# Strassen's seven products on six k-tiles of the feed-forward input instead of four, plain units mixed among them, and the activations split in the output stage

## The reference

```
x = x + 0.5 * SwiGLU_1(rms_norm(x))          # w_in 2048 x (2*5632), w_out 5632 x 2048
h = rms_norm(x); P = h @ w_in                # q, k, v of 8 dilated and 8 differential heads
x = x + concat(attention heads) @ w_out
x = x + 0.5 * SwiGLU_2(rms_norm(x))

def swiglu_ffn(x, g, w_in, w_out):
    h = rms_norm(x, g)
    gate, up = jnp.split(h @ w_in, 2, axis=-1)
    return (jax.nn.silu(gate) * up) @ w_out
```

## Time and profile before

| quantity | value |
|---|---|
| median of three runs | 1860.8 us |
| profiled execution, its own time | 1861.02 us |
| its span | 1859.2 us |
| PE, DVE, ACT busy | 1842.5, 1254.9, 941.3 us |
| DMA | 352.88 MB, 190 GB/s mean |

### The profile page before, as it was taken

One profiled execution on the slowest core, in us unless ns is written; L12 is line 12 of the kernel. 1 busy time (PEld: TensorE's weight loads), 2 busy tenths in 40 slices (PEclk: granted clock), 3 DMA queues, 4 the chain that ended last, 5 costly groups with the idle time before them and its releaser, 6 DMA issues.

```text
span 1859.2 us, 23201 instructions
## 1 busy us (share of the span) xinstructions
PE 1842.5 (99%) x8408; PEld 1529.2 (82%) x8408; DVE 1254.9 (67%) x1432; ACT 941.3 (51%) x1183; POOL 47.8 (3%) x71
## 2 busy tenths in 40 slices
PE   7999999999999999999999999999999999999999
PEld 6888888888888888888888888888888888888887
...
PEclk9999999999999999999999999999999999999999
...
GB/s 296 170 202 198 208 182 205 200 196 188 226 182 180 187 203 198 189 183 155 174 167 181 138 172 167 163 200 209 195 204 201 185 209 193 203 181 182 193 214 114
DMA packets 178888, 352.88 MB, mean 190 GB/s; under 512 B 7312, under 2 KB 7952, under 8 KB 178576
## 3 DMA queue, kind: packets, MB, share of 16 engines
...
...
## 4 chain that ended last, share of the span: by engine, by line
PE 98%; DVE 1%; DMA 0%; ACT 0%; issue 0%; SPq 0%; ACTq 0%
PE acc L391 22%; PE acc L393 22%; PE acc L392 22%; PE acc L495 6%; PE acc L496 6%; PE acc L494 6%; PE turn L435 2%; PE turn L433 2%; PE turn L434 2%; PE turn L418 2%; PE acc L435 1%; PE acc L434 1%; PE acc L433 1%; PE turn L546 1%; PE turn L567 1%; DMA w_raw<-in_ffn_w_in 0%
## 5 line engine op out<-in xcount | busy, mean ns | idle before, releaser
L894 DVE TENSOR_TENSOR w_lo<-w_raw,w_hi 128x1024 fp32r<-128x1024 f32 x352 | 413.2, 1182 | 395.6 <-ACT w_hi L649 393.3
L649 ACT ACTIVATE w_hi<-w_raw 128x1024 fp32r<-128x1024 f32 x352 | 358.7, 1021 | 460.0 <-PE acc L393 439.6
L663 ACT ACTIVATE w_hi<-w_raw 128x1024 fp32r<-128x1024 f32 (+1 forms) x400 | 402.9, 1017 | 363.6 <-PE acc L496 131.3
L903 DVE TENSOR_TENSOR w_lo<-w_raw,w_hi 128x1024 fp32r<-128x1024 f32 (+1 forms) x400 | 460.4, 1168 | 151.6 <-ACT w_hi L663 146.1
L391 PE MATMUL acc<-w_hi,h_hi 128*128 128x512 f32 x992 | 392.1, 395 | 1.8 <-DVE w_lo L894 1.8
L393 PE MATMUL acc<-w_hi,h_lo 128*128 128x512 f32 x992 | 387.1, 390 | 0.0
L392 PE MATMUL acc<-w_lo,h_hi 128*128 128x512 f32 x992 | 386.9, 390 | 0.0
L391 PE MATMUL acc<-w_hi,act_hi 128*128 128x512 f32 x704 | 274.3, 390 | 0.0
L393 PE MATMUL acc<-w_hi,act_lo 128*128 128x512 f32 x704 | 273.9, 389 | 0.0
L392 PE MATMUL acc<-w_lo,act_hi 128*128 128x512 f32 x704 | 273.9, 389 | 0.0
L391 PEld LDWEIGHTS acc<-w_hi,h_hi 128*128 128x128 f32 x992 | 186.8, 188 | 42.0 <-issue 4.8
...
## 6 DMA issues: line engine op xcount, KB each, us to landing
w_raw<-in_ffn_w_in SPq DMA_DIRECT2D x176, 1024.0 KB, 5.0
w_raw<-in_ffn_w_out SPq DMA_DIRECT2D x64, 1024.0 KB, 4.9
w_raw<-in_w_in SPq DMA_DIRECT2D x48, 1024.0 KB, 5.0
...
w_raw<-in_w_out SPq DMA_DIRECT2D x16, 1024.0 KB, 4.9
...
```

What stands on the lines that cost most here:

```text
L649: nc.scalar.activation(w_hi[:, v % RING, 0:count, :], w_raw[:, v // 2 % RAW, k0:k0 + count, :], ACT.Copy).then_inc(hi_ready, 1)
L663: nc.scalar.activation(w_hi[:, v % RING, 0:count, :], w_raw[:, piece % RAW, k0:k0 + count, :], ACT.Copy).then_inc(hi_ready, 1)
L894: nc.vector.tensor_tensor(w_lo[:, v % RING, 0:count, :], w_raw[:, v // 2 % RAW, k0:k0 + count, :], w_hi[:, v % RING, 0:count, :].bitcast(F32),
L903: nc.vector.tensor_tensor(w_lo[:, v % RING, 0:count, :], w_raw[:, piece % RAW, k0:k0 + count, :], w_hi[:, v % RING, 0:count, :].bitcast(F3 ...
```

## The change

Each half of the Strassen block has three k-tiles instead of two (`KS = 3`), and ten k-tiles stay plain (`K_PLAIN`). A product is now two units, of 2 and of 1 k-tile, with 9 matmuls in all. An iteration has 24 units: 10 plain ones (120 matmuls) and 14 units of products (63 matmuls), 183 in all. `IN_RAW` lists them in order: four plain, P1, P5, a plain one, P2, P6, two plain, P3, P4, P7, three plain.

The raw blocks of the products now have their own buffer, `block_raw`, with five places of 3 k-tiles. Two plain k-tiles of gate and of up go to `odd_raw`. The four weight sums are made with other operands, are 1536 columns wide instead of 1024, and stand at other places of DVE's order. The DMAs of an iteration are ten instead of eight, with the same bytes.

`block_raw`, `s_hi` and `s_lo` lie where `act_hi` lies. So while the input stage runs, hidden activations are only copied (`copy_act`, ACT) to `act_raw`, which is `act_lo`'s memory. They are split later (`round_act`): blocks 0 and 1 in the last iteration, blocks 2 to 9 among the first chunk's units. PE waits for this by `act_ready`. The last iteration is written out behind the loop on ACT and DVE. The factor `rstd` of the up half moves out of `hidden` and into `update_x` (`half_rstd`).

In `activation_sums` the token operands are made from `h_hi + h_lo` with one sum of 1536 columns and four of 384.

```
-IN_UNITS = 20
+KS = 3
+K_PLAIN = KD - 2 * KS
...
+G0, G1, U0, U1, G2, U2, B11, B12, B21, B22, T1 = range(11)
+IN_RAW = ((G0, 0, 2), (G0, 2, 2), (G1, 0, 2), (G1, 2, 2), (B11, 0, 2), (B11, 2, 1), (T1, 0, 2), (T1, 2, 1), (G2, 0, 2),
+          (B21, 0, 2), (B21, 2, 1), (T1, 0, 2), (T1, 2, 1), (U0, 0, 2), (U0, 2, 2), (B22, 0, 2), (B22, 2, 1),
+          (B21, 0, 2), (B21, 2, 1), (B12, 0, 2), (B12, 2, 1), (U1, 0, 2), (U1, 2, 2), (U2, 0, 2))
+IN_UNITS = len(IN_RAW)
+P1, P5, P2, P6, UP, P3, P4, P7, UP_REST = 4, 6, 9, 11, 13, 15, 17, 19, 21
+SUM_OF = {P5: 1, P5 + 1: 1, P6: 2, P6 + 1: 2, P4: 3, P4 + 1: 3, P7: 4, P7 + 1: 4}
+FREED = {G0: 2, G1: 4, B11: 6, G2: 9, U0: 15, B22: 17, B21: 19, B12: 21, U1: 23, U2: 24}
...
+            s_hi = sb("s_hi", [P, 4, KS, P], F32R, sums)
+            s_lo = sb("s_lo", [P, 4, KS, P], F32R, sums)
+            block_raw = sb("block_raw", [P, 5, KS, NC], F32, sums)
+            sums.enter_context(nc.sbuf_tensor("sums_end", [P, KF * SEQ - 2 * 4 * KS * P - 5 * KS * NC], F32))
+            act_raw = sb("act_raw", [P, KF, SEQ], F32, sums)
...
+                for piece in FREED:
+                    if not first:
+                        sp.wait_ge(lo_ready, i * IN_UNITS + (base + FREED[piece]))
+                    elif piece < G2:
+                        sp.wait_ge(lo_ready, UNIT[s_in] + 2 * (piece + len(PARTS_D) + 1))
+                    elif piece in (G2, U2):
+                        sp.wait_ge(rows_ready, ROWS[R_FFN1 if s_in == IN1 else R_FFN2])
+                    elif s_in == IN2:
+                        sp.wait_ge(units_used, UNIT[s_in])
...
+            def form(u0, p, lhs, o, start, stop):
+
+                for v in (p, p + 1):
+                    count = IN_RAW[v][2]
+                    pe.wait_ge(lo_ready, u0 + v + 1)
+                    for kk in range(count):
...
-                for v in range(4, 6):
-                    in_unit(u0, v, 2 * v, UK, 0, False, False)
+                turn_rows(i + r0, 0, splits(r0), None, i + r0)
                 if s_in == IN2:
                     pe.wait_ge(bank_free[2], READS[s_in][2])
-                form(u0, P1, block_of(KD - 4, 0), partial[0], True, True)
+                form(u0, P1, block_of(0, 0), partial[0], True, True)
                 form(u0, P5, sum_of(1), partial[1], True, True)
-                form(u0, P2, block_of(KD - 2, 0), banks[0][:, 0, :], False, True)
+                in_unit(u0, P2 - 1, 2 * KT, 0, (True, True), False)
+                form(u0, P2, block_of(1, 0), banks[0][:, 0, :], False, True)
                 pe.wait_ge(partial_copied, copies + 1)
                 form(u0, P6, sum_of(2), partial[0], True, True)
-                form(u0, P4, block_of(KD - 2, 1), banks[0][:, 1, :], False, True)
-                form(u0, P3, sum_of(4), banks[1][:, 0, :], True, False)
+                for v in range(UP, P3):
+                    in_unit(u0, v, UK * (v - UP), 1, (v > UP, v > UP), False)
+                form(u0, P3, sum_of(4), banks[1][:, 0, :], False, False)
+                form(u0, P4, block_of(1, 1), banks[0][:, 1, :], False, True)
                 pe.wait_ge(partial_copied, copies + 2)
                 form(u0, P7, sum_of(3), partial[0], True, True)
...
+                for v in range(UP_REST, IN_UNITS):
+                    in_unit(u0, v, UK * (v - UP_REST + P3 - UP), 1, (True, True), v == IN_UNITS - 1)
...
+                    for v in range(UNITS_F):
+                        if v == 4 and b < turns:
+                            r = i * 2 + (r0 + IN_LOOPS + b)
+                            turn_rows(r, b, r - (b + IN_LOOPS * (n + 1)), None, r - b)
+                        if v < UNITS_A and v % 2 == 0:
+                            pe.wait_ge(act_ready, IN_LOOPS * n + ACT_NEEDED[v])
+                        if v == UNITS_A:
+                            pe.wait_ge(turn_split, splits(r0 + FFN_ITERS))
+                        chunk(PARTS_F, u0, range(v, v + 1), act, b)
...
+            def copy_act(i, r0):
+
+                act.wait_ge(rows_turned, i + (r0 + 1))
+                nc.scalar.activation(act_raw[:, bass.ds(i * 4, 4), :], turn4[0], ACT.Copy).then_inc(turn_hi, 1)
+
+            def round_act(j):
+
+                nc.scalar.activation(act_hi[:, KT * j:KT * (j + 1), :], act_raw[:, KT * j:KT * (j + 1), :],
+                                     ACT.Copy).then_inc(act_hi_ready, 1)
...
+            def hidden(s_in, i, r0, n):
+
+                split_in_hi(s_in, i, n, 4, 8)
+                copy_act(i, r0)
                 split_in_hi(s_in, i, n, 8, 10)
                 copy_partial(s_in, i)
-                split_in_hi(s_in, i, n, 10, 18)
+                split_in_hi(s_in, i, n, 10, 27)
                 silu(s_in, i)
-                split_in_hi(s_in, i, n, 18, 24)
+                if isinstance(i, int):
+                    for j in range(2):
+                        round_act(j)
+                split_in_hi(s_in, i, n, 27, 28)
...
+                    if c == 0:
+                        round_act(2)
...
+            def round_act(n, j):
+
+                dve.wait_ge(act_hi_ready, IN_LOOPS * n + j + 1)
+                k = slice(KT * j, KT * (j + 1))
+                nc.vector.tensor_tensor(act_lo[:, k, :], act_raw[:, k, :], act_hi[:, k, :].bitcast(F32),
+                                        ALU.subtract).then_inc(act_ready, 1)
...
+                landed = i * 16 + (IN_LOOPS * n + 1) * 16
+                b_11, b_12, b_21, b_22, t_1 = (in_raw(piece) for piece in (B11, B12, B21, B22, T1))
+                dve.wait_ge(block_landed[0], landed)
+                dve.wait_ge(block_landed[1], landed)
+                weight_sum(t_1, b_12, b_11, ALU.subtract)
+                split_in_lo(s_in, i, 4, 9)
+                dve.wait_ge(block_landed[3], landed)
+                dve.wait_ge(sum_ready, sums + 1)
+                dve.wait_ge(lo_ready, i * IN_UNITS + (u0 + P5 + 2))
+                weight_sum(t_1, b_22, t_1, ALU.subtract)
+                split_in_lo(s_in, i, 9, 14)
+                dve.wait_ge(sum_ready, sums + 2)
+                dve.wait_ge(lo_ready, i * IN_UNITS + (u0 + P2 + 2))
+                weight_sum(b_21, b_21, t_1, ALU.subtract)
+                split_in_lo(s_in, i, 14, 15)
+                weight_sum(b_12, b_22, b_12, ALU.subtract)
+                split_in_lo(s_in, i, 15, 17)
+                dve.wait_ge(units_used, i * IN_UNITS + (u0 + P6 + 2))
                 dve.wait_ge(partial_copied, copies + 1)
                 add(rows[:, 1, 0, :], partial[0], rows[:, 0, 0, :]).then_inc(partial_copied, 1)
-                split_in_lo(s_in, i, 13, 16)
-                dve.wait_ge(units_used, i * IN_UNITS + (u0 + P7 + 1))
+                split_in_lo(s_in, i, 17, 25)
+                dve.wait_ge(units_used, i * IN_UNITS + (u0 + P7 + 2))
                 dve.wait_ge(partial_copied, copies + 2)
                 add(rows[:, 0, 1, :], partial[0], rows[:, 1, 0, :]).then_inc(partial_copied, 1)
                 add(rows[:, 1, 0, :], partial[1], rows[:, 1, 0, :])
-                split_in_lo(s_in, i, 16, 17)
                 dve.wait_ge(partial_copied, copies + 3)
                 add(rows[:, 1, 1, :], partial[1], rows[:, 0, 1, :]).then_inc(partial_added, 1)
                 dve.wait_ge(partial_added, done)
                 add(rows[:, 0, :, :], acc[0][:, :, :], rows[:, 0, :, :]).then_inc(bank_free[0], 1)
-                split_in_lo(s_in, i, 17, 24)
+                split_in_lo(s_in, i, 25, 28)
+                if isinstance(i, int):
+                    for j in range(2):
+                        round_act(n, j)
                 dve.wait_ge(units_used, i * IN_UNITS + (u0 + IN_UNITS))
                 add(rows[:, 1, :, :], acc[1][:, :, :], rows[:, 1, :, :]).then_inc(up_ready, 1)
                 dve.wait_ge(up_ready, done)
                 dve.wait_ge(gated, done)
...
+                nc.vector.tensor_tensor(rows[:, 0, :, :], rows[:, 0, :, :], rows[:, 1, :, :],
+                                        ALU.mult).then_inc(rows_ready, 1)
...
+                    by = 1.0 if stage == PROJ else half_rstd[:, t:t + 1]
+                    s = nc.vector.scalar_tensor_tensor(o, banks[bank][:, t, :], by, o, ALU.mult, ALU.add)
...
+                with dve.Fori(0, IN_LOOPS - 1) as i:
+                    hidden(s_in, i, n)
+                hidden(s_in, IN_LOOPS - 1, n)
                 for c in range(4):
                     first = c * UNITS_F
-                    split_lo(s_out, first + 4, first + 8, PARTS_F)
+                    if c == 0:
+                        round_act(n, 2)
+                        split_lo(s_out, 4, 6, PARTS_F)
+                        round_act(n, 3)
+                        split_lo(s_out, 6, 8, PARTS_F)
...
                     if c == 0:
                         turn_split_lo(r, act_hi, act_lo, KF - 4, 0)
+                        for j in range(4, IN_LOOPS):
+                            round_act(n, j)
+                            split_lo(s_out, 2 * j, 2 * j + 2, PARTS_F)
```

(17 more changed lines are left out.)

219 lines of the change are left out of this document (95 added, 124 removed).

## The result

The changed kernel takes 1874.0 us (median of 4 runs, 1872.6 to 1874.8), the kernel before, run beside it, 1860.6 us. The ratio is 1.0069, with a 95% interval of 1.0057 to 1.0081: slower, by 13 us. Forecast were 1866.6 us and a range of 1857.5 to 1873 us. Its profiled execution took 1873.9 us with a span of 1872.0.

A forecast was written before the change was run, and what follows sets the result against it. PE was taken to set the time: 1861.0 - 13.6 (matmuls) + 9.0 (iteration waits) + 10.4 (seams) = 1866.8 us for a profiled execution, so 1866.6 us as median; range 1857.5 to 1873 us.

The forecast's parts named there:

- Matmuls, -13.6 us: PE, input stage: three matmuls fewer in each of 20 iterations, 60 x 0.227 = 13.6 us less if PE stays fed.
- Wait in the iteration, +9.0 us: PE waits 0.45 us for the low part of unit 17, 20 times: 9.0 us, 0 to 20 us in all.
- the walk: Step-by-step count of DVE's work from unit 0's start: low part of unit 17 starts at 29.25 us, PE ready at 30.2.
- Wait at the seam, +10.4 us: Input to output stage: PE waits for activation block 0's low part, 3.8 to 5.5 us per seam; two seams, 10.4 us.
- T + 2.75: Seam: DVE starts the low part of the last weights 2.75 us after T, the end of PE's last input-stage unit.
- rival B: Seams: the gap of 5 us lowers PE's clock, 2.1 us more per seam, 1870.8 us; 25 in 100.
- The sign given for it: Profile: PEclk at 9 in all slices, unless the rival of a falling clock at the seams holds.
- The first block, put at nothing: First block: activation_sums grows by about 2 us, covered by three units ahead (8 us); uncovered, 4 us for both layers.
- A: Iterations: DVE fits, a wide sum costs 1.5 us or less, only the seams cost: 1857.6 us; 22 in 100.
- D: Iterations and seams: neither wait shows, as releases come otherwise than read: 1847.2 us; 3 in 100.
- C: Iterations: DVE later still, 1.83 us per wide sum and a dearer restart, wait 0.9 us: 1875.6 us; 8 in 100.
- The output stage's first chunk, put at nothing: First output chunk: eight more low parts on DVE (9.1 us) and eight high parts on ACT cost PE nothing.

The follow-up runs named there:

- The last kernel of the experiments: Changed kernel with the seam's splits forward on both engines, the sum b_12 early and the activation sums one unit later: 1851.45 us, 0.9945 against the kernel before.
- the kernel with the filled gap: Changed kernel with 22 extra 512-column matmuls on PE at each seam, ahead of the wait for act_lo(0), into an unread bank: 1869.7 us.
- The experiment with the later sums: Changed kernel with the activation sums one unit later in the first block, on DVE and ACT: 1873.5 us.
- the eleven profiles: Changed kernel's own profile (1873.9 us) and ten others with this block's code unchanged; the block took 44.41 to 46.2 us.

## Why the prediction was wrong

The direction held, and so did the waits for VectorE, by which the forecast was above the kernel before. The time was 7.4 us too low: the sum had no term for the clock behind the seams, 4.0 to 4.3 us. The clock alone would have given about 1871 us; the rest came from the iterations and the first block. By the steps of the sum:

- **Matmuls, -13.6 us: right.** 60 fewer, still 0.227 us apart. The last kernel of the experiments keeps 10 of these 13.6 us.
- **Wait in the iteration, +9.0 us: right place, too small.** A wide sum takes 1.66 us to the next start (421.81 to 423.47), 1.67 by the forecast. VectorE came to the low part of unit 17 when the walk says: 435.48 is 29.24 us behind the start of unit 0 (406.24), the walk has 29.25. PE came there later than forecast, so it lost 0.27 us instead of 0.45. But the row of 60 has two more units in each iteration that are met just too late; they cost 0.05 us each, and matmuls here and there hundredths. Together an iteration of 42.92 us holds 0.53 us over 183 x 0.2267 + 0.9 = 42.39, which is 10.6 us for 20. I had walked one unit and taken all others as in time: 1.6 us of the miss. That it is so little is partly luck: of the 9.0 us put on unit 17 it took 5.4, and 5.2 came from places without a term.
- **Wait at the seam, +10.4 us: right.** 5.30 and 5.16 us, 10.5 in all, by the path that the prediction walked. The row of DVE at 494.90 is its T + 2.75 with T = 492.2.
- **The clock at the seam, put into rival B: this step failed.** The forecast took the matmuls behind the gap at full clock. They ran at the 1.2 GHz level, 11 and 8 slow starts, which cost 2.5 + 1.6 = 4.1 us by the profile's rows, 4.0 us by the seams of the kernel with the filled gap and 4.3 us by its time. B was held at 25 in 100 beside the forecast; it belonged in the sum. The sign given for it, PEclk below 9 in a slice, could not have shown it: B came true with 9 in all of them. In the profiles of this kernel and its variants, all 12 seams with a wait of 3.8 us or more had slow matmuls behind them. The one stretch that bore on it, the slow matmuls behind the start's wait, had been there, and I had set against it that the start was PE's first work. The Trainium skill (TensorE: Matmul & The Clock Gate, on HAM oscillation) states that long idle gaps bring the clock down; the trace agrees, with 0.43 us between starts behind 5.3 us. B's price of 2.1 us per seam was right: 2.5 and 1.6 were measured.
- **The first block, put at nothing: wrong in this profile.** I said that three units, 8 us, cover `activation_sums`. They don't cover it when weights land late (over 4.0 us of wait at ACT).

Timeline of DVE, ACT and PE of the changed kernel in the first layer's first block.

```profile
35.63 2.01 ACT L691 ACTIVATE w_hi<-w_raw 128x1024 fp32r<-128x1024 f32 x2 [5.23 <-DMA w_raw<-in_ffn_w_in]
...
37.93 1.75 DVE L1077 TENSOR_TENSOR rows<-h_hi,h_lo 128x1536 f32<-128x1536 f32 x1
...
41.85 1.22 DVE L955 TENSOR_TENSOR w_lo<-w_raw,w_hi 128x1024 fp32r<-128x1024 f32 x1
41.97 1.49 ACT L768 ACTIVATE s_hi<-block_raw 128x1536 fp32r<-128x1536 f32 x1 [4.33 <-DVE block_raw L1081]
...
43.12 0.50 PE L431 MATMUL acc<-w_hi,h_hi 128*128 128x512 f32 x1 [0.30 <-DVE w_lo L955]
```

ACT had waited 5.2 us for a load, so that nothing was ahead when DVE went into 3.9 us of sums. The next low part starts at 41.85, and PE is 0.57 us late at 43.12 and again 3.3 us later: +1.2 us here, nothing in the second layer. The experiment with the later sums did not test the cure, but the eleven profiles show the cause. Whether the change makes this load later than it was before is open: the kernel before has one profile, with 3.7 us of wait at this place.

Together 4.1 + 1.6 + 1.2 = 6.9 us, of the 7.1 between the sum for a profiled execution, 1866.8, and the one of the changed kernel, 1873.9. Rivals A and D fall with the waits; C does too, since its 0.9 us per iteration was not there. The output stage's first chunk, put at nothing, was nothing: 60.73 us from its first transposes to the next in both kernels.

One sum of the prediction is off in itself: 0.2 to 0.5 us per iteration and 4.4 to 5.4 us per seam give 1860.0 to 1868.0 us, not the 1862 to 1869 that it names as the forecast's own range. The measured time lies above both.
